# Expert loop of a hybrid encoder block: a prefetch hint for the closing branch on every engine

## The reference

```python
def moe_ffn(h, router_w, router_b, w_up, b_up, w_down, b_down):
    # top-4 of 32 experts per token, softmax over the four logits, rows sorted by expert
    ...
    def expert_block(args):
        xb, e = args
        gu = xb @ w_up[e] + b_up[e]
        x_glu = jnp.minimum(gu[:, :D_FF_EXPERT], SWIGLU_LIMIT)
        x_lin = jnp.clip(gu[:, D_FF_EXPERT:], -SWIGLU_LIMIT, SWIGLU_LIMIT)
        hid = x_glu * jax.nn.sigmoid(SWIGLU_ALPHA * x_glu) * (x_lin + 1)
        return hid @ w_down[e] + b_down[e]
```

## Time and profile before

| | |
|---|---|
| median of 3 runs | 2402.25 us (2398.61 to 2404.02) |
| the profiled execution, its own time | 2401.52 us |
| its span, first to last instruction | 2399.8 us |
| mean granted TensorE clock | 0.963 |
| PE busy | 2210.7 us, 92% |
| DVE busy | 1785.6 us, 74% |
| ACT busy | 1268.3 us, 53% |
| POOL busy | 354.9 us, 15% |
| first turn starts on PE | 968 us |
| last working turn ends, empty turns on PE | about 2328 to 2344 us |

### The profile page before, as it was taken

The page is one execution under the profiler, slowest core; times in us unless marked ns, Lnnn a source line. Parts: engine busy times, 40 slices in busy tenths (PEclk is TensorE's granted clock), DMA queues, the critical chain, the costliest instruction groups (busy, mean ns, idle before and its releaser), DMA issues.

```text
span 2399.8 us, 42146 instructions
## 1 busy us (share of the span) xinstructions
PE 2210.7 (92%) x14912; PEld 1761.7 (73%) x14913; DVE 1785.6 (74%) x2010; ACT 1268.3 (53%) x1427; POOL 354.9 (15%) x307
## 2 busy tenths in 40 slices
PE   5999988599989978899999999999999999999983
PEld 4789966498857966777777777777777777877752
DVE  5499897625043266899898898889988888988872
ACT  5412264513142125667766666666666666766642
POOL 0000000020003101222221221121221212212210
PEclk9999998799999969999999999999999999999996
DMA  4211231221101035989988898899898989989864
GB/s 151 70 53 36 81 98 40 98 84 36 53 18 32 27 122 204 356 309 341 375 306 311 296 329 301 275 329 328 307 318 291 323 300 331 375 298 325 293 190 171
DMA packets 260532, 514.90 MB, mean 215 GB/s; under 512 B 11365, under 2 KB 45338, under 8 KB 260098
## 3 DMA queue, kind: packets, MB, share of 16 engines
q1 hardware_dynamic: 245266, 467.28, 54.5%
q0 software_dynamic: 13280, 43.56, 7.4%
q10 hardware_dynamic: 1904, 2.90, 0.5%
HBM read 476.33 MB, written 37.36 MB: 214 GB/s over the span
## 4 chain that ended last, share of the span: by engine, by line
PE 70%; DVE 10%; issue 7%; DMA 7%; ACT 4%; SPq 0%; DVEq 0%; POOLq 0%; ACTq 0%; POOL 0%
PE PS L2763 11%; PE PS L2764 10%; PE PS L2249 10%; PE PS L2766 8%; DMA raw<-in_exp_w_up 6%; PE PS L2790 5%; PE PS L2652 4%; PE PS L2504 4%; DVE wlo L2029 3%; PE PS L2755 3%; ACT whi L1233 2%; PE PS L2726 2%; PE PS L2778 2%; PE PS L2606 1%; PE PS L2575 1%
## 5 line engine op out<-in xcount | busy, mean ns | idle before, releaser
L2029 DVE TENSOR_TENSOR wlo<-raw,whi 128x2048 fp32r<-128x2048 f32 x384 | 869.1, 2285 | 131.8 <-ACT whi L1233 109.7
L1233 ACT CAST whi<-raw 128x2048 fp32r<-128x2048 f32 x384 | 726.5, 1912 | 170.1 <-DMA raw<-in_exp_w_up 73.9
L2763 PE MATMUL PS<-whi,xhi 128*128 128x512 f32 x1024 | 425.3, 415 | 4.5 <-DVE wlo L2029 4.5
L2764 PE MATMUL PS<-wlo,xhi 128*128 128x512 f32 x1024 | 400.7, 391 | 0.0
L2766 PE MATMUL PS<-whi,xlo 128*128 128x512 f32 x768 | 301.8, 393 | 0.0
L2763 PEld LDWEIGHTS PS<-whi,xhi 128*128 128x128 f32 x1024 | 194.1, 190 | 46.9 <-DVE wlo L2029 10.4
L2763 PE MATMUL PS<-whi,hhi 128*128 128x512 f32 x512 | 206.8, 404 | 21.4 <-issue 15.7
L2764 PEld LDWEIGHTS PS<-wlo,xhi 128*128 128x128 f32 x1024 | 193.4, 189 | 39.2
L2764 PE MATMUL PS<-wlo,hhi 128*128 128x512 f32 x512 | 200.4, 391 | 0.0
L2766 PEld LDWEIGHTS PS<-whi,xlo 128*128 128x128 f32 x768 | 144.8, 189 | 32.1
L2766 PE MATMUL PS<-whi,hlo 128*128 128x512 f32 x384 | 150.7, 392 | 0.0
(11 more groups left out here) (417 smaller groups left out, 4310.9 us busy)
## 6 DMA issues: line engine op xcount, KB each, us to landing
raw<-in_exp_w_up SPq DMA_DIRECT2D x256, 1024.0 KB, 9.9
raw<-in_exp_w_down SPq DMA_DIRECT2D x128, 1024.0 KB, 7.6
ring<-in_w_in SPq DMA_DIRECT2D x11, 1024.0 KB, 5.3
xres<-in_x SPq DMA_DIRECT2D x4, 1024.0 KB, 10.3
ring<-in_xattn_wk SPq DMA_DIRECT2D x4, 1024.0 KB, 9.1
ring<-in_xattn_wv SPq DMA_DIRECT2D x4, 1024.0 KB, 6.3
ring<-in_w_out SPq DMA_DIRECT2D x4, 1024.0 KB, 12.8
xres<-in_x SPq DMA_DIRECT2D x2, 2048.0 KB, 8.5
```

Of the source, the lines that this page charges most:

```text
L1233: nc.scalar.copy(whi[:, chunk_slot(c, NSPL), :], raw[chunk_slot(c, NRAW)][:]).then_inc(s_whi, 1)
L2029: nc.vector.tensor_tensor(wlo[:, chunk_slot(c, NSPL), :], raw[chunk_slot(c, NRAW)][:], whi[:, chunk_slot(c, NSPL), :].bitcast(F), ALU.subtract
L2763: pe.matmul(o, hi[:, k, :], wh, start=k == 0 and bias is None, stop=False)
L2764: pe.matmul(o, hi[:, k, :], wl, start=False, stop=False)
```

## The change

```diff
@@ sync
-            with sp.Fori(1, NVIS + 1) as t:
+            with nc.Fori(1, NVIS + 1, engines=(mybir.EngineType.SP,), hint_back_edge=True) as t:
@@ gpsimd
-            with pool.Fori(1, NVIS + 1) as t:
+            with nc.Fori(1, NVIS + 1, engines=(mybir.EngineType.Pool,), hint_back_edge=True) as t:
@@ scalar
-            with act.Fori(1, NVIS + 1) as t:
+            with nc.Fori(1, NVIS + 1, engines=(mybir.EngineType.Activation,), hint_back_edge=True) as t:
@@ vector
-            with dve.Fori(1, NVIS + 1) as t:
+            with nc.Fori(1, NVIS + 1, engines=(mybir.EngineType.DVE,), hint_back_edge=True) as t:
@@ tensor
-            with pe.Fori(1, NVIS + 1) as t:
+            with nc.Fori(1, NVIS + 1, engines=(mybir.EngineType.PE,), hint_back_edge=True) as t:
```

## The result

| | before | after |
|---|---|---|
| median | 2402.25 us | 2410.66 us (2409.51 to 2412.15, 5 runs) |
| ratio | | 1.0038, 95% interval 1.0024 to 1.0052 |
| the profiled execution, its own time | 2401.52 us | 2409.51 us |
| its span | 2399.8 us | 2407.8 us |

What follows compares the result with a forecast made beforehand. PE was taken to bound the loop, busy 98% of the working turns, with the empty turns serial on it. 2.2 + 1.1 + 0 = +3.3 us gave 2404.8 us profiled, 2405.5 on the median; range 2399.5 to 2413.

Steps and rivals of the forecast that it cites:

- Rival 2: The hinted closing branch on PE gets cheap: about -1 us, 2401, or 2396.5 if the hint costs nothing; chance 0.12.
- rival 3: Unrecorded fetches at PE's closing branches in working turns, which the hint removes: up to 40 us faster, say 2375; chance 0.03.
- Term 1: 22 empty turns on PE behind the working turns: the hint adds 0.099 us each, +2.2 us, bounds 2.0 and 3.2.
- Term 2: Tops of the 31 working turns: PE late in 22, 2.2 us, half taken: +1.1 us, bounds nothing and 4.5.
- Term 3: What the hint could give back: no instruction fetches in the loop, so nothing to prefetch, 0 us.
- rival 1: In empty turns the hint fetches code already held, closing branches wait: 11 to 29 us more, middle 2425; chance 0.12.

Runs made afterwards that it cites:

- run 1: The hint on PE's loop alone, against the kernel before: 2407.13 us against 2401.73, ratio 1.002.
- run 6: The hint on PE alone, moved behind the `If` so only the 31 working turns run it, against the kernel before: 2404.8 us against 2402.32, ratio 1.0011.
- run 7: No hint, loop ended at the last visit on all engines (no empty turns), against the kernel before: 2390.14 us against 2402.32, ratio 0.995.
- run 10: No hint, three satisfied waits at the top of PE's turn, against the kernel before: 2406.64 us against 2402.66, ratio 1.0019.
- run 8: No empty turns, with the hint on all five engines, against the kernel before: 2392.89 us against 2402.32, ratio 0.9962.
- run 9: The changed kernel measured again, unaltered, against the kernel before: 2409.26 us against 2402.66, ratio 1.0027.
- run 2: The hint on SP, POOL, ACT and DVE, none on PE, against the kernel before: 2403.37 us against 2401.73, ratio 1.0007.
- run 3: The hint on DVE alone, against the kernel before: 2402.06 us against 2401.73, ratio 1.0.
- run 4: One satisfied wait in place of the hint on all engines, against the kernel before: 2401.25 us against 2401.73, ratio 0.9998.
- run 5: No hint, one plain register instruction at the top of PE's turn, against the kernel before: 2401.74 us against 2402.32, ratio 1.0002.

## Why the prediction was right on the way and the range, and short on the size

The forecast was +3.3 us. The measured +8.4 and +6.6 us lie inside the range of 2399.5 to 2413, but the first lies beyond the 7.7 us that the sum's own bounds allow: it is the 3 us added for the spread of runs that took it in, so the range held in part by luck. Which way, where and on which engine was forecast rightly; the size was short in all three terms.

**The bound, the place and the sign: right.** The working turns are bound by PE, the empty turns stand between them and the last visit, and 22 sequencer turns on PE are serial. Runs 1, 6, 7 and 10 move this gap the way that this mechanism says. That nothing is fetched from the second working turn to the end of the empty ones is right as well, and with it that the hint could bring nothing: PE's closing branch got slower, not faster. Rivals 2 and 3 fall on PE. Rival 2's effect does exist on ACT and DVE, where the closing branch got 56 and 16 ns cheaper, less than the hint itself costs there. That the other engines hide behind PE was right: with the hint DVE's turn is 0.81 us, PE's 0.87.

**Term 1, the empty turns: 2.2 forecast, 2.9 measured.** The hint's own slot was well priced by the row of the ALU_OP: 0.090 us measured, 0.099 taken. The step that was short is the unspoken one that the other instructions of the turn would keep their price. Both branches grew, by 19 and 17 ns, and with the hint's slot the turn grew by 0.13. It lies inside the bounds given (2.0 to 3.2).

**Term 2, the tops of working turns: 1.1 forecast, between 2 and 4 measured.** The reading of the earlier trace rows was right: in 22 turns the sequencer is late. Two steps were mis-sized. The path of the sequencer from L2840, behind the body, to L2832 of the next turn grew by 0.15 us (mean of 30, 0.93 to 1.09), not by 0.099, since it holds the slowed branches; and 25 tops are late instead of 22. The idle time at the tops grew by 4.3 us. How much of it reaches the end is not settled. By the medians, less than all: run 1 leaves 5.4 - 2.9 = 2.5 us for it, run 6 2.5 - 0.3 = 2.2, runs 8 and 7 2.75 - 1 = 1.8, and run 9 6.6 - 2.9 - 1.0 = 2.7, each with an interval of 2 us or more to either side. By the profiles, about all: the working turns, measured as above, took 1362.2, 1360.0, 1363.1, 1362.8 and 1360.7 us in five with PE's hint in them (the changed kernel and runs 1, 6, 8 and 9) and 1359.4, 1356.6, 1359.7, 1356.6, 1355.8 and 1358.0 in six without (before and runs 2 to 5 and 7). The means differ by 4.1 us, with a spread of 3 to 4 within a kind; run 10 lies between, at 1360.2. The prediction had taken half without a run to show it, and its reason was misread: the chain of before runs through a weight transfer of 12 to 13 us at the top of nine turns, not five. The earlier trace rows lists the longest pieces alone, not all of them.

**Term 3, zero forecast, about 1 measured.** This is the step that failed: from "nothing is fetched in the loop" the prediction concluded that a hint has no effect on fetches. It had looked at the turns from 1010 us on the earlier trace rows and not at what was fetched ahead in the first of them: the block behind the loop. With the hint this fetch does not take place there: one packet of q8 and three of q14 are missing. On DVE it comes back as a wait of 2.7 to 2.9 us in the last stage (runs 2, 3, 8, 9), of which all but about one don't reach the end. On PE the displaced fetch shows no wait: the packet moves at 2351.8 us, 1.1 us after the first matmul behind the loop, and PE is not idle again from there to its last matmul. This was a weaker relative of rival 1: not a fetch too many, but one too late. Rival 1 itself falls: no instruction packet moves between 1012 us and the end of the empty turns, but for the displaced one of run 6.

**The sum.** With the medians' 2.5 us for term 2 it is 2.9 + 2.5 + 1.0 = 6.4 us, with the profiles' 4.1 it is 8.0. Measured are 6.6 in run 9 (3.8 to 8.9 by its interval) and 8.4 in the first comparison (5.8 to 12.5). Both intervals hold both sums. That the five hints together cost more than their parts is not shown. The outcome that the prediction held likeliest, no change within 0.2% (0.61), did not come: with the slower branches, the tops and the fetch the sum crosses that line.

## What to carry to other kernels

Before a loop is given a branch hint, look in the trace for instruction packets inside it and for a closing branch that is now and then much longer than its median. Here there was none, and on the engine that bounds the loop the hint only cost: its slot in every turn, slower branches, and a later fetch of what follows the loop. Look at the fetches of the loop's first turn as well, since code behind the loop can be among them. And look at what a sequencer does in turns without work: here 22 empty turns cost 12.2 us (run 7), more than the whole change, and an end of the loop that follows the data takes them away.

## What the runs showed of the hardware

- A sequencer instruction is not free on TensorE where the sequencer is late to feed the engine: one satisfied wait of 51 ns at the top of a turn cost 4.0 us over 53 turns (run 10), 2.4 of them in 22 empty turns and the rest at the tops of working turns.
- A single wait or register operation added at the same place got no slot of its own on PE and cost nothing that could be measured (runs 4 and 5: 0.5 and 0.6 us below the kernel before, inside their intervals).
- While a hint is armed, branches take longer: on PE 214 to 233 ns for the closing branch and 213 to 230 for the `If`, on ACT 50 to 98 ns for the `If`. After the last hint this lasted for two passes of the hinted branch and went (run 6). On ACT the hinted branch with the gap behind it got shorter, 257 to 201 ns.
- An armed hint held back the next fetch of its engine, once and for the length of the loop, though nothing was fetched for the hint's own target. The fetch came when the hint had ceased to act (run 6: 2337.2 us) or behind the loop (the changed kernel: 2351.8 us on PE, 2392.8 on DVE).
- A fetch that came too late cost DVE a wait of 2.7 to 2.9 us, though the packet, of 8 KB, was under way for only 0.33.
